# Two attentions walked by pairs of heads, with the softmax division moved behind the weighting

## The reference, cut to what matters

```
def _neighborhood_attention(h, w_qkv, rpb, w_o):      # 4 rows x 64 columns of tokens
    ...
        s = jnp.einsum('bqhd,bkqjhd->bhqkj', q_r, k_g).astype(jnp.float32) + bias.astype(jnp.float32)
        p = jax.nn.softmax(s.reshape(B, NA_HEADS, GRID_W, kh * kw), axis=-1)
    ...
    return o @ w_o

def _mla(h, w_down, q_norm, w_uq, kv_norm, w_ukv, w_o):
    ...
    scale = (MLA_NOPE + MLA_ROPE) ** -0.5             # 96 ** -0.5
    ...
        s = (jnp.einsum('bqhd,bkhd->bhqk', qn, k_nope)
             + jnp.einsum('bqhr,bkr->bhqk', qr, k_rope)).astype(jnp.float32) * scale
        p = jax.nn.softmax(s, axis=-1).astype(v.dtype)
        return jnp.einsum('bhqk,bkhd->bqhd', p, v)
    ...
    return o @ w_o
```

## Time and profile before

| | |
|---|---|
| median of 3 runs | 1633.93 us (1631.55 to 1639.19) |
| span of the profiled execution | 1626.9 us; the time around it is not in the profile, and the median lies 7.0 us above the span |
| PE busy | 1572.8 us, 97% |
| DVE busy | 1203.0 us, 74% |
| ACT busy | 864.5 us, 53% |
| POOL busy | 116.5 us, 7% |
| the chain that ended last | PE 87%, DVE 7%, ACT 4% |
| neighbourhood attention, first score matmul to first matmul of its projection | 687.86 to 744.24 us |
| latent attention, the same | 1017.02 to 1065.02 us |

### The profile page before, as it was taken

One profiled execution on the slowest core, in us unless ns is written; L12 is line 12 of the kernel. 1 busy time (PEld: TensorE's weight loads), 2 busy tenths in 40 slices (PEclk: granted clock), 3 DMA queues, 4 the chain that ended last, 5 costly groups with the idle time before them and its releaser, 6 DMA issues.

```text
span 1626.9 us, 24767 instructions
## 1 busy us (share of the span) xinstructions
PE 1572.8 (97%) x10292; PEld 1359.5 (84%) x10292; DVE 1203.0 (74%) x1428; ACT 864.5 (53%) x1009; POOL 116.5 (7%) x138
## 2 busy tenths in 40 slices
PE   8999999989999999998999999999999999999998
PEld 7999979877999999946999986578888888888886
DVE  6767769755777776455777672658898998997997
ACT  5343456443443344344433442447777777777775
POOL 0100012210000000062000001710000000000000
PEclk9999999989999999999999999999999999999999
DMA  8877634212687764504777750028998998998983
GB/s 346 293 277 264 251 107 153 72 56 96 261 324 296 278 251 156 181 1 172 286 271 261 272 196 23 1 104 311 370 344 321 366 342 319 368 346 326 368 331 142
DMA packets 51921, 386.30 MB, mean 237 GB/s; under 512 B 5888, under 2 KB 6224, under 8 KB 7904
## 3 DMA queue, kind: packets, MB, share of 16 engines
q1 hardware_dynamic: 50400, 376.16, 62.3%
q0 software_dynamic: 1408, 8.54, 1.4%
HBM read 383.63 MB, written 1.05 MB: 236 GB/s over the span
## 4 chain that ended last, share of the span: by engine, by line
PE 87%; DVE 7%; ACT 4%; issue 1%; DMA 1%; POOL 1%; DVEq 0%; ACTq 0%
PE bank L302 24%; PE bank L304 23%; PE bank L303 23%; PE bank L1289 4%; DVE sb_wlo L269 2%; PE bank L1864 2%; PE bank L1823 1%; ACT sb_whi L265 1%; PE bank L1854 1%; PE bank L699 1%; PE bank L2026 1%; PE bank L1986 1%; DVE sb_ada_acc L689 1%; PE bank L2333 1%; PE bank L2367 1%
## 5 line engine op out<-in xcount | busy, mean ns | idle before, releaser
L269 DVE TENSOR_TENSOR sb_wlo<-sb_raw,sb_whi 128x2048 fp32r<-128x2048 f32 x137 | 313.9, 2293 | 171.4 <-ACT sb_whi L265 171.1
L302 PE MATMUL bank<-sb_xhi,sb_whi 128*128 128x256 f32 x1344 | 382.6, 285 | 4.9 <-DVE sb_xlo L585 2.8
L304 PE MATMUL bank<-sb_xhi,sb_wlo 128*128 128x256 f32 x1344 | 380.8, 283 | 0.0
L303 PE MATMUL bank<-sb_xlo,sb_whi 128*128 128x256 f32 x1344 | 380.8, 283 | 0.0
L265 ACT ACTIVATE sb_whi<-sb_raw 128x2048 fp32r<-128x2048 f32 x137 | 261.4, 1908 | 175.2 <-PE bank L304 171.7
L302 PEld LDWEIGHTS bank<-sb_xhi,sb_whi 128*128 128x128 f32 x1344 | 258.0, 192 | 9.2 <-issue 5.2
L303 PEld LDWEIGHTS bank<-sb_xlo,sb_whi 128*128 128x128 f32 x1344 | 258.0, 192 | 1.1
L304 PEld LDWEIGHTS bank<-sb_xhi,sb_wlo 128*128 128x128 f32 x1344 | 258.0, 192 | 0.0
L2297 DVE TENSOR_TENSOR sb_wlo<-sb_raw,sb_whi 128x2048 fp32r<-128x2048 f32 x84 | 191.0, 2289 | 12.5 <-ACT sb_whi L2291 12.0
L302 PE MATMUL bank<-sb_whi,sb_slots_hi 128*128 128x512 f32 x448 | 181.6, 405 | 0.0
L304 PE MATMUL bank<-sb_whi,sb_slots_lo 128*128 128x512 f32 x448 | 176.2, 393 | 0.0
(11 more groups left out here) (462 smaller groups left out, 2492.3 us busy)
## 6 DMA issues: line engine op xcount, KB each, us to landing
sb_raw<-in_ffn SPq DMA_DIRECT2D x98, 1024.0 KB, 4.9
sb_raw<-in_moe SPq DMA_DIRECT2D x86, 1024.0 KB, 6.7
sb_ada_raw<-in_ada SPq DMA_DIRECT2D x32, 1536.0 KB, 6.4
sb_cst<-in_moe SPq DMA_DIRECT2D x28, 1024.0 KB, 6.9
sb_xn<-in_moe SPq DMA_DIRECT2D x27, 1024.0 KB, 7.0
sb_ada_raw<-in_moe SPq DMA_DIRECT2D x27, 1024.0 KB, 6.9
sb_raw<-in_w_in SPq DMA_DIRECT2D x13, 1024.0 KB, 4.8
sb_raw<-in_na_qk SPq DMA_DIRECT2D x8, 1024.0 KB, 5.0
```

Of the source, the lines that this page charges most:

```text
L269: e.tensor_tensor(wlo[s][:, :], raw[s][:, :], whi[s][:, :], ALU.subtract).then_inc(s_lo[s], 1)
L302: e.matmul(dst, wh, xh, start=first, stop=False, skip_group_check=skip)
L303: e.matmul(dst, wh, xl, start=False, stop=False, skip_group_check=skip)
L304: return e.matmul(dst, wl, xh, start=False, stop=last, skip_group_check=skip)
```

## The change

- `attend` goes by pairs of heads, `n` from 0 to 9, with three stages that lie one pair apart. Masks and scores of the two heads alternate; so do the matmuls of the two heads in `weigh`.
- The exponentials are not normalised. They are transposed as they are; `weigh` gives the unnormalised result in columns 0 to 255 of its bank, and four matmuls ahead of it (L1880) spread the reciprocals of the row sums over 64 partitions for each head into columns 256 to 511. ScalarE copies the plain result out (L1890) and VectorE multiplies it by the spread reciprocals (L1896). GpSimd's multiplications are gone.
- The copy of transposed blocks goes to ScalarE for the even head (L1872) and stays on VectorE for the odd head (L1874).
- The latent attention's scale is multiplied into the table by which the queries are multiplied anyway; the reduction gives the maximum with its sign turned, so the small instruction that did both is gone there.
- There are four buffers for exponentials instead of three; they, one buffer for transposed blocks and two for plain results lie in a part of `cst` (`late`) that holds constants of the mixer.

```
-    attn |= {"turned": both, "cos": cos, ...}
+    attn |= {"turned": both * np.float32(QH) ** -0.5, "cos": cos, ...}
...
+    s = [env["h"][:, :, :], env["sil"][:, :, :], blocks(0), blocks(NB * T)]
+    pt = [env["rstd"][:, :, :], blocks(2 * NB * T)]
+    part = lambda i, q: bank[i % 2][:, q * T:(q + 1) * T]
+
+    def score(n):
+        for q in range(NB):
+            if mask is not None:
+                for i in both(n):
+                    pe.step(lambda e, i=i, q=q: e.matmul(part(i, q), *mask(i), start=True, stop=False),
+                            *m_ready(i), m_sread.get(i - 2))
+            for i in both(n):
+                m_score[i] = pe.step(lambda e, i=i, q=q: e.matmul(part(i, q), *scores(i, q), start=mask is None, stop=True),
+                                     *m_ready(i), m_sread.get(i - 2))
+
+    def largest(n):
+        if bias is None:
+            for i in both(n):
+                src = bank[i % 2][:, :].rearrange("p (q t) -> p q t", q=NB)
+                m_max[i] = dve.step(lambda e, i=i, src=src: e.reduce_max(mx[:, i, 0:2], src, AX_X, negate=True), m_score[i])
+            return
+        for i in both(n):
+            for q in range(NB):
+                m = dve.step(lambda e, i=i, q=q: e.tensor_tensor_reduce(
+                    s[i % 4][:, q, :], part(i, q), bias[:, q, i, :], 1.0, -3e38, ALU.add, ALU.max,
+                    mx[:, i, q:q + 1]), m_score[i], m_tr.get(i - 4))
+            m_sread[i] = m
+            m_max[i] = dve.step(lambda e, i=i: e.tensor_scalar(mx[:, i, 0:2], mx[:, i, 0:2], -1.0, None, ALU.mult), m)
+
+    def exponentials(n):
+        for i in both(n):
+            for q in range(NB):
+                m_exp[i] = act.step(lambda e, i=i, q=q: e.activation(
+                    s[i % 4][:, q, :], s[i % 4][:, q, :] if bias is not None else part(i, q), ACT.Exp,
+                    bias=mx[:, i, q:q + 1], accum_out=mx[:, i, 2 + q:3 + q]), m_max[i], m_tr.get(i - 4))
+            if bias is None:
+                m_sread[i] = m_exp[i]
...
-    def normalised(i):
-        m3 = dve.step(lambda e: e.reciprocal(mx[:, i, 2:4], mx[:, i, 2:4]), m_exp[i])
-        for q in range(NB):
-            m3 = pool.step(lambda e, q=q: e.tensor_scalar(s[i % 3][:, q, :], s[i % 3][:, q, :], mx[:, i, 2 + q:3 + q],
-                                                          None, ALU.mult), m3)
...
+    def kept(i):
+        src = bank[2 + i % 2][:, :].rearrange("p (k q) -> p k q", k=NB)
+        if i % 2 == 0:
+            m_pt[i] = act.step(lambda e: e.activation(pt[0], src, ACT.Copy), m_tr[i], m_pv.get(i // 2 - 1))
         else:
+            m_pt[i] = dve.step(lambda e: e.tensor_copy(pt[1], src), m_tr[i], m_pv.get(i // 2 - 1))
+
+    def weigh(n):
+        bk = bank[4 + n % 2]
         for q in range(NB):
+            for i in both(n):
+                pe.step(lambda e, q=q, i=i: e.matmul(
+                    bk[i % 2 * HD:(i % 2 + 1) * HD, T + q * P:T + (q + 1) * P],
+                    mx[:, i, 2 + q:3 + q].broadcast_to([P, HD]), ident, start=True, stop=True), m_rec[n], m_out.get(n - 2))
         for kb in range(NB):
+            for i in both(n):
+                m = pe.step(lambda e, kb=kb, i=i: e.matmul(bk[i % 2 * HD:(i % 2 + 1) * HD, 0:T], values(i, kb), pt[i % 2][:, kb, :],
+                                                           start=kb == 0, stop=kb == NB - 1), m_pt[i], m_out.get(n - 2))
+        m_pv[n] = m
...
+    for n in range(pairs + 2):
+        if n < pairs:
+            score(n)
+        if n >= 2:
+            weigh(n - 2)
+            plainly(n - 2)
+        if n < pairs:
+            largest(n)
+        if 0 <= n - 1 < pairs:
+            inverse(n - 1)
+            transposed(n - 1)
+            kept(2 * n - 2)
+        if n >= 2:
+            scaled(n - 2)
+        if 0 <= n - 1 < pairs:
+            kept(2 * n - 1)
+        if n < pairs:
+            exponentials(n)
+        if n >= 2 and n % 2:
+            at = n - 3
+            parts += env["split_pair"](at, m_out[at], m_out[at + 1])
+        follow(2 * n)
+        follow(2 * n + 1)
```

More of the change, by code:

```diff
@@ L111, in shape_constants @@
             placeturn[swap[i], at + i] = sign[i]
-    attn |= {"turned": both, "cos": cos, "sin": sin, "place": place, "placeturn": placeturn}
+    attn |= {"turned": both * np.float32(QH) ** -0.5, "cos": cos, "sin": sin, "place": place, "placeturn": placeturn}
     def pack(parts):
@@ L1803, in backwards, with attend @@
     return bass.AP(tensor=ap.tensor, offset=ap.offset + step * (n - 1), ap=[*ap.ap[:-1], [-step, n]])
[L1806 to L1812, removed]
+def attend(env, ctx, tag, scores, values, bias, m_ready, follow, mask=None, order=None):
+    sb, bank, pe, act, dve = (env[n] for n in ("sb", "bank", "pe", "act", "dve"))
+    ident, y, late = env["ident"], env["xn"], env["late"]
+    pairs = AH // 2
+    blocks = lambda at: late[:, at:at + NB * T].rearrange("p (b t) -> p b t", b=NB)
+    s = [env["h"][:, :, :], env["sil"][:, :, :], blocks(0), blocks(NB * T)]
+    pt = [env["rstd"][:, :, :], blocks(2 * NB * T)]
+    plain = [late[:, 3 * NB * T + i * T:3 * NB * T + (i + 1) * T] for i in range(2)]
@@ L1813, in attend @@
     mx = sb(f"mx_{tag}", [P, AH, 4], ctx=ctx)
[L1814 to L1818, removed]
+    m_score, m_max, m_exp, m_sread, m_tr, m_pt, m_rec, m_pv, m_plain, m_out = ({} for _ in range(10))
+    both = lambda n: (2 * n, 2 * n + 1)
+    part = lambda i, q: bank[i % 2][:, q * T:(q + 1) * T]
+    def score(n):
         for q in range(NB):
             if mask is not None:
[L1821 to L1825, removed]
-            for q in range(NB):
[L1827 to L1830, removed]
-        else:
[L1832 to L1835, removed]
@@ new lines, in exponentials, with inverse @@
+    def exponentials(n):
[6 more added lines that the diff above has]
+                m_sread[i] = m_exp[i]
+    def inverse(n):
+        at = 2 * n
+        m_rec[n] = dve.step(lambda e: e.reciprocal(mx[:, at:at + 2, 2:4], mx[:, at:at + 2, 2:4]), m_exp[at + 1])
@@ new lines, in transposed @@
+    def transposed(n):
+        for i in both(n):
+            bk = bank[2 + i % 2]
+            for kb in range(NB):
+                for q in range(NB):
+                    m = pe.step(lambda e, kb=kb, q=q, bk=bk, i=i: e.transpose(
+                        bk[:, kb * T + q * P:kb * T + (q + 1) * P], s[i % 4][:, q, kb * P:(kb + 1) * P], ident),
+                        m_exp[i], m_pt.get(i - 2))
+            m_tr[i] = m
+    def kept(i):
+        src = bank[2 + i % 2][:, :].rearrange("p (k q) -> p k q", k=NB)
+        if i % 2 == 0:
+            m_pt[i] = act.step(lambda e: e.activation(pt[0], src, ACT.Copy), m_tr[i], m_pv.get(i // 2 - 1))
+        else:
+            m_pt[i] = dve.step(lambda e: e.tensor_copy(pt[1], src), m_tr[i], m_pv.get(i // 2 - 1))
@@ L1850, in transposed @@
-    def transposed(i):
-        bk = bank[2 + i % 2]
-        for kb in range(NB):
[L1853 to L1871, removed]
@@ L1873, in split @@
-    def split(n):
-        return env["split_pair"](2 * n, *[m_out[2 * n + z] for z in range(2)])
-    parts = []
[L1877 to L1889, removed]
-        follow(i)
@@ L1891, in attend @@
-    return parts + split(AH // 4 - 1)
+            for i in both(n):
+                pe.step(lambda e, q=q, i=i: e.matmul(
+                    bk[i % 2 * HD:(i % 2 + 1) * HD, T + q * P:T + (q + 1) * P],
+                    mx[:, i, 2 + q:3 + q].broadcast_to([P, HD]), ident, start=True, stop=True), m_rec[n], m_out.get(n - 2))
+        for kb in range(NB):
+            for i in both(n):
+                m = pe.step(lambda e, kb=kb, i=i: e.matmul(bk[i % 2 * HD:(i % 2 + 1) * HD, 0:T], values(i, kb), pt[i % 2][:, kb, :],
+                                                           start=kb == 0, stop=kb == NB - 1), m_pt[i], m_out.get(n - 2))
@@ new lines, in weigh, with plainly, scaled @@
+        m_pv[n] = m
+    def plainly(n):
+        m_plain[n] = act.step(lambda e: e.activation(plain[n % 2], bank[4 + n % 2][:, 0:T], ACT.Copy), m_pv[n], m_out.get(n - 2))
+    def scaled(n):
+        dst, a, b = y[:, n, :], plain[n % 2], bank[4 + n % 2][:, T:2 * T]
+        if order is not None:
+            dst, a, b = order(dst), *(z.rearrange("p (r c) -> p r c", c=GRID) for z in (a, b))
+        m_out[n] = dve.step(lambda e: e.tensor_tensor(dst, a, b, ALU.mult), m_plain[n], m_pv[n])
+    parts = []
@@ L1894, in neighbourhood @@
+    return parts
 def neighbourhood(env, early, m_in):
```

10 lines of the change are left out of this document (2 added, 8 removed).

## The result

The changed kernel takes 1637.71 us (median of 20 runs, 1632.74 to 1640.62) against 1633.62 us (20 runs, 1627.26 to 1639.19) for the kernel before: ratio 1.0024, 95% interval 1.0015 to 1.0034. It is slower by 3.9 us, where 15 us less were forecast, and 1637.7 lies above the range of 1610 to 1630.

A forecast was written before the change was run, and what follows sets the result against it. TensorE was taken to bound both attentions. Neighbourhood -15.4 and latent +0.4 gave -15.0 us, span 1626.9 to 1611.9, and with the median 7.0 above the span 1619 us; range for 8 in 10, 1610 to 1630.

The forecast's parts named there:

- all four gate matmuls fall into PE's idle time: Latent attention: the gate matmuls fit into the 1.6 us that PE idles in each pair of 6.0 us.
- gate to 695.2, then pair 2 with a gate, 3.75 + 0.96: Neighbourhood attention's ramp: gate matmul ends at 695.2, next pair takes 3.75 plus 0.96 for its gate, PE done at 699.9.
- the whole ring: Latent attention: chain through PE and ScalarE from one pair's exponentials to the next's, 6.0 us a pair against 4.92 before.
- no gap around the gate matmuls: Latent attention: a sign that the forecast is right, beside starts of pairs' scores 6.0 us apart.
- Rival C: Clock falls in the ramp as before, or at a new place in one ramp: 3 to 4 us back, 1622.5; 15%.
- Two for one on halves: Matmuls on different array halves run at once: neighbourhood masks and scores 1.08 instead of 2.16 us, values 0.86 instead of 1.72.
- rival A: Halves don't overlap in these shapes, in both attentions: +26 us, 1645, slower than before; chance 7%.
- Switches of the shape: PE's work in each pair: changing matmul shape costs 0.10 us before the spread and 0.16 after the values.
- Neighbourhood attention: Window: ramp 12.0, then 4.9, 3.8, 5.2, 3.8, 5.2, tail 6.1; together 41.0 instead of 56.4 us, -15.4.
- The stall before pair 7: Neighbourhood attention: PE stalls 1.4 us before scores of pairs 5 and 7, maxima standing behind the split's low part.
- Latent attention: Window: pair 1 ends after 8.7, six rings 36.0, tail 3.6; together 48.4 instead of 48.0 us, +0.4.
- The offset of 7.0 us between span and median: Whole kernel: the median stands 7.0 us above the span, taking span 1611.9 to 1619 us.

The follow-up runs named there:

- experiment 1: The changed kernel with follow(2n), ScalarE's copy of the gate row and GpSimd's product, called at the head of a pair, ahead of its exponentials: 1614.90 us, ratio 0.9886.
- the last kernel: experiment 1 plus latent scores by head, latent transposes and copies ahead of the scores, and the split's low part behind the maxima in both attentions: 1604.61 us, ratio 0.9830.
- Experiment 4: experiment 1 with spread and values of a pair's two heads separated by the transposes of the next pair's even head: 1635.71 us, ratio 1.0018.
- Spread alone: The kernel before, head by head, with only the normalisation moved behind the weighting (spread matmuls, no GpSimd products): 1633.12 us, ratio 1.0002.
- experiment 3: experiment 1 with spread and values of a pair in order of heads, all of the even head, then all of the odd: 1617.56 us, ratio 0.9902.

## Why the prediction was wrong

The step that failed is the gate's. The prediction said "all four gate matmuls fall into PE's idle time", and in the ramp "gate to 695.2, then pair 2 with a gate, 3.75 + 0.96". It priced the matmul L1042 at its own 0.96 us and never asked what that matmul waits for. Its bank comes free with L1046, and L1046 stood among the rows of ScalarE's order that I showed, behind the four exponentials. In the kernel before the copy of a gate row stood one head away from the next gate matmul (even head and odd head); by pairs the two stand in the same place, with 2.0 us of exponentials just ahead. The matmul's delay held the next pair's scores, and with them the whole ring. This cost 21 us in the windows, of which 6.6 are the clock's half speed, and turned -17 into +4. Two of the prediction's own signs show it: it wanted "no gap around the gate matmuls", and it named a clock under 1.00 as a sign of being wrong. Rival C had the clock fall once, at a ramp, for 3 to 4 us; it fell four times, each time behind this wait.

Point by point, with experiment 1 as the kernel that has no such wait:

- Two for one on halves: right. In the last kernel's rows the spread of both heads takes 0.49 us and their values 0.96 to the transposes. Experiment 4 built most of rival A (forecast 1645, measured 1636; masks and scores, 8.6 us of the rival's sum, stayed paired in it).
- Switches of the shape: 0.10 us. In the same rows eight score records of 0.215 end their steps at 1024.27, and the spread starts at 1024.37. From the values to the transposes it is the same: 0.96 us less four steps of 0.215. The prediction took 0.10 for the first and 0.16, the price of a full drain, for the second, so the second was priced 0.06 too high.
- Neighbourhood attention: ramp 12.06 us (689.73 to 701.79; forecast 12.0), pair with gate 4.53 (4.9), pair without 3.67 (3.8), pairs 5 to 7 together 13.0 (14.2), tail 5.5 (6.1). Window 38.8 instead of 41.0. The stall before pair 7 cost 1.4 us as forecast, that before pair 5 only 0.6 (forecast 1.4 too); by my reading because a gate matmul, 0.96 us, stands ahead of pair 4's scores and gives the low part that time.
- Latent attention: pair 1's exponentials end 8.6 us after the start (8.7), six rings are 36.7 (36.0), tail 3.4 (3.6); window 48.7 (48.4, though its terms add to 48.3). Right, and the gate falls into the idle time once its bank is free.
- Spread alone: 0.44 us a head (0.43), while ramps and tails together give back 8.9 us in the neighbourhood attention and 5.3 in the latent one. PE's waits for GpSimd before were 5.7 and 3.6 us; in the first, 1.1 us of a wait for ScalarE came in their place.
- The offset of 7.0 us between span and median was two things. In one and the same execution the time stands 1.8 us above the span (1636.1 and 1634.3 in the changed kernel, 1614.86 and 1613.1 in experiment 1). The other 5.2 were that the profiled execution of before was a quick one. It did no harm here, since it was added to both sides.

With that wait out, the forecast's -15.0 stands against -16.9 in the windows and -18.6 [-21.4, -16.0] by the ratio: no term of the two sums was off by more than 1.2 us, and the one that was missing was larger than their total.

## What to carry to other kernels

When a loop is regrouped, list for every engine each instruction that moves, also those of side work that "only fills gaps", and ask of each which buffer it frees and who is queued behind the one that needs it: 0.6 us of copying was worth 22.8 us. Work on halves of TensorE's array overlaps when it stands side by side in the queue, in whichever order inside the group. After a stage is halved look for the ring that goes through the other engines: putting the short chain (scores, maximum, exponentials) alone between two of its own turns took, with the scores by head, the latent beat from 6.1 to 4.3 us.

## What was not expected of the hardware

- TensorE started matmuls of the upper half of the columns beside those of the lower half although two whole matmuls of the lower half were queued ahead of them (713.32, against 713.74 for the second of the two). The Trainium skill (TensorE: Matmul & The Clock Gate, Part 3: Packing small matmuls) says that matmuls start and end strictly in program order; the starts in these rows disagree for different halves, and so does the time of experiment 3. Across transposes that use the whole array it did not reach (experiment 4).
- The granted clock of the changed kernel fell to half behind waits of 2.36, 2.65, 3.17 and 3.30 us and stayed full behind others of 2.65 and 2.78 us. In experiment 4 it fell once (0.71 over 1050 to 1055 us) where the wait ahead was only 1.29 us, and stayed full behind another of 1.29 in the pair before. The length of the wait alone doesn't tell which, and what does is open. Each of these falls cost 1.6 to 1.7 us.
